# Three attention loops with the turn two blocks behind the scores and projection steps shared out one by one

## What is computed

```python
s_f = einsum('bhqd,bhkd->bhqk', qf, k_f) * scale_f
s_f = s_f + cf[..., :, None] - cum_f[..., None, :]
p_f = softmax(where(causal, s_f, -inf)); o_f = einsum('bhqk,bhkd->bhqd', p_f, v_f)
s_d = einsum('bhcqd,bhckd->bhcqk', qd, k_d) * scale_d
p_d = softmax(where(causal, s_d, -inf))
a_d = p_d[:, :, 0] - lam * p_d[:, :, 1]; o_d = einsum('bhqk,bhkd->bhqd', a_d, v_d)
```

## Time and profile before

| what | us |
|---|---|
| runs of before | 3536.08 median (3534.78 to 3537.95) |
| profiled execution | 3540.3 |
| its span, first to last instruction | 3538.2 |
| PE busy in it | 3451.2 |
| DVE, ACT, POOL busy | 1223.9, 1256.6, 1522.4 |
| first, second attention loop and third block's loop (scores, first to last) | 1704 to 1869, 2711 to 2876, 3395 to 3501 |

### The profile page before, as it was taken

The page is one execution under the profiler, slowest core; times in us unless marked ns, Lnnn a source line. Parts: engine busy times, 40 slices in busy tenths (PEclk is TensorE's granted clock), DMA queues, the critical chain, the costliest instruction groups (busy, mean ns, idle before and its releaser), DMA issues.

```text
span 3538.2 us, 39182 instructions
## 1 busy us (share of the span) xinstructions
PE 3451.2 (98%) x16124; PEld 2779.6 (79%) x16124; DVE 1223.9 (35%) x2100; ACT 1256.6 (36%) x1924; POOL 1522.4 (43%) x709
## 2 busy tenths in 40 slices
PE   7999999999999999999999999999999999999998
PEld 3777887887888887887777888888887778888776
DVE  3165683631221135212554111121113651111544
ACT  4433323432322332223454222232223553222544
POOL 2422353666444444445414444444445234444332
PEclk8999999999999999999999999999999999999999
DMA  6211133442233323333112223232332122233211
GB/s 231 95 54 54 58 116 101 155 155 89 96 129 135 99 95 131 141 98 102 62 32 88 99 97 95 95 101 96 92 102 87 34 75 89 96 95 99 68 65 54
DMA packets 98719, 341.19 MB, mean 96 GB/s; under 512 B 11308, under 2 KB 11564, under 8 KB 98125
## 3 DMA queue, kind: packets, MB, share of 16 engines
q1 hardware_dynamic: 97632, 334.02, 28.4%
q10 hardware_dynamic: 908, 4.67, 0.3%
HBM read 336.02 MB, written 2.10 MB: 96 GB/s over the span
## 4 chain that ended last, share of the span: by engine, by line
PE 91%; DVE 3%; ACT 3%; POOL 1%; issue 1%; DMA 1%; ACTq 0%; DVEq 0%; POOLq 0%
PE ps L1156 25%; PE ps L1158 25%; PE ps L1157 25%; PE ps L1175 2%; PE ps L1176 2%; PE ps L1177 2%; PE ps L1444 2%; PE ps L1471 1%; PE ps L1457 1%; PE ps L1359 1%; POOL t L2612 1%; PE ps L1230 1%; DMA t<-in_w_f1i 1%; DMA t<-in_xT 1%; DVE t L2102 1%
## 5 line engine op out<-in xcount | busy, mean ns | idle before, releaser
L2612 POOL TENSOR_TENSOR t<-t,t 128x1024 fp32r<-128x1024 f32 (+2 forms) x588 | 1363.7, 2322 | 1792.6 <-ACT t L1539 1791.6
L1156 PE MATMUL ps<-t,t 128*128 128x512 f32 (+1 forms) x4048 | 1606.1, 397 | 22.8 <-POOL t L2612 14.2
L1158 PE MATMUL ps<-t,t 128*128 128x512 f32 (+1 forms) x4048 | 1583.1, 391 | 0.0
L1157 PE MATMUL ps<-t,t 128*128 128x512 f32 (+1 forms) x4048 | 1578.2, 390 | 0.0
L1156 PEld LDWEIGHTS ps<-t,t 128*128 128x128 f32 x4048 | 763.5, 189 | 190.6 <-issue 18.8
L1158 PEld LDWEIGHTS ps<-t,t 128*128 128x128 f32 x4048 | 762.1, 188 | 167.3
L1157 PEld LDWEIGHTS ps<-t,t 128*128 128x128 f32 x4048 | 763.1, 189 | 157.6 <-issue 1.4
L1539 ACT CAST t<-t 128x1024 fp32r<-128x1024 f32 (+2 forms) x588 | 583.9, 994 | 567.5 <-PE ps L1158 423.1
L2405 DVE TENSOR_TENSOR t<-t,ps 128x512 f32<-128x512 f32 x110 | 75.7, 688 | 528.9 <-PE ps L1158 514.0
L1606 ACT CAST t<-t 128x512 fp32r<-128x512 f32 x158 | 97.0, 621 | 404.0 <-DVE t L2405 358.2
L1793 ACT ACTIVATE t<-t 128x512 f32<-128x512 f32 x88 | 55.6, 632 | 317.9 <-DVE t L2398 317.8
(11 more groups left out here) (282 smaller groups left out, 2357.0 us busy)
## 6 DMA issues: line engine op xcount, KB each, us to landing
t<-in_w_f1i SPq DMA_DIRECT2D x88, 512.0 KB, 3.3
t<-in_w_f2i SPq DMA_DIRECT2D x88, 512.0 KB, 3.3
t<-in_w_ada SPq DMA_DIRECT2D x72, 512.0 KB, 4.5
t<-in_w_ffi SPq DMA_DIRECT2D x44, 512.0 KB, 3.7
t<-in_w_f1o SPq DMA_DIRECT2D x32, 512.0 KB, 3.5
t<-in_w_f2o SPq DMA_DIRECT2D x32, 512.0 KB, 3.5
t<-in_w_gate SPq DMA_DIRECT2D x24, 512.0 KB, 3.9
t<-in_w_out SPq DMA_DIRECT2D x48, 256.0 KB, 2.7
```

Of the source, the lines that this page charges most:

```text
L1156: e.matmul(out, wh[:, at], X.hi[c][:, 0:N], start=c == first, stop=False)
L1157: e.matmul(out, wh[:, at], X.lo[c][:, 0:N], start=False, stop=False)
L1158: m = e.matmul(out, wl[:, at], X.hi[c][:, 0:N], start=False, stop=c == final)
L2612: e.tensor_tensor(k.WL[:, n % NHL, 0:w], k.raw[:, j % NRAW, 0:w], f(k.WH[:, n % NHL, 0:w]), ALU.subtract).then_inc(*k.rest.inc(('rest', j) ...
```

## The change

In `attend`, for pairs (Fox and third block), one iteration becomes: weigh (scored-1), scores (n), turn of every weighed job up to two behind the scores, a step of `beside`, gather of what was turned, and a second step when `due` allows. `due` grows by `rate` per iteration, 1.0 in the second block and 1.6 in the third, and by 2.0 after the last scores. The number of jobs by which the turn lags is 1 behind the weighed in this phase and 0 after the last scores. For differential heads the branches are written anew. At the crossing to Fox heads the two waiting differential turns come before one step, and up to four gathers after it.

The second yield of each `outd` tile is dropped. In GLA `outer` becomes `outers`: for both directions it first takes the banks and waits for keys and values, and then emits the two matmuls.

```diff
@@ -664,7 +664,7 @@
         self.N = ring(k, 'N ' + tag, k.tmp[3:], since) if tag != 'm' else None
         first = 1 if tag == 'm' else 0
         self.stats = ring(k, 'stats ' + tag, [k.sm[:, 8 * i:8 * i + 8] for i in range(first, first + 8)], since)
-        self.out = 0
+        self.out, self.rate = (0, 1.6 if tag == 'm' else 1.0)
 
     def parts(self, h):
 
@@ -702,35 +702,45 @@
 def attend(on, at, beside):
 
     scored = weighed = turned = gathered = 0
-    total = len(at.jobs)
-    pair = lambda j: at.jobs[j][0][0] != 'd'
-    while gathered < total:
-        if scored < total and pair(scored):
-            if weighed < scored:
-                on.weigh(at, *at.jobs[weighed])
-                weighed += 1
-            on.scores(at, *at.jobs[scored])
-            scored += 1
-        elif scored < total:
-            on.scores(at, *at.jobs[scored])
-            scored += 1
-        if turned > gathered and (pair(gathered) or turned - gathered > 1 or scored == weighed == turned):
+    total, due = (len(at.jobs), 0.0)
+
+    def gather(until):
+        nonlocal gathered
+        while gathered < until:
             h, qt = at.jobs[gathered]
             on.gather(at, h, qt)
             gathered += 1
             if qt == 3:
                 on.head_out(at, h)
                 at.out += 1
-        if weighed < scored and (scored == total or scored - weighed > 1):
+    while gathered < total:
+        pair = scored == total or at.jobs[scored][0][0] != 'd'
+        if pair and weighed < scored:
             on.weigh(at, *at.jobs[weighed])
             weighed += 1
-        two = turned < total and pair(turned)
-        if two:
-            next(beside, None)
-        if weighed > turned and (two or weighed - turned > 2 or scored == weighed):
+        if scored < total:
+            on.scores(at, *at.jobs[scored])
+            scored += 1
+        if not pair:
+            gather(turned - 1)
+            if scored - weighed > 1:
+                on.weigh(at, *at.jobs[weighed])
+                weighed += 1
+        lag = 2 if not pair else 1 if scored < total else 0
+        while turned < weighed - lag:
             on.turn(at, *at.jobs[turned])
             turned += 1
-        next(beside, None)
+        if not pair:
+            next(beside, None)
+            continue
+        due += at.rate if scored < total else 2.0
+        if due >= 1.0:
+            due -= 1.0
+            next(beside, None)
+        gather(turned)
+        while due >= 1.0:
+            due -= 1.0
+            next(beside, None)
     for _ in beside:
         pass
 
@@ -801,7 +811,6 @@
         for n in range(KT):
             on.T(('outd_' + L, n), 'out' + L, n, at.OA, kt=4, first=4)
             on.part(res, n, ('outd_' + L, n))
-            yield
             yield
 
     def norms():
@@ -1330,8 +1339,7 @@
     def chain_begin(self, h):
         for v in range(2):
             self.take(self.k.banks, 'bo', h, v, hold=True)
-        for d in range(2):
-            self.outer(h, 0, d)
+        self.outers(h, 0)
 
     def intra(self, h):
         k, e = (self.k, self.e)
@@ -1344,8 +1352,8 @@
 
     def chain(self, h, step):
         k, e = (self.k, self.e)
-        for d in range(2 if step < 6 else 0):
-            self.outer(h, step + 1, d)
+        if step < 6:
+            self.outers(h, step + 1)
         for d in range(2):
             c = step if d == 0 else 7 - step
             at = slice(64 * c, 64 * c + 64)
@@ -1363,14 +1371,18 @@
         for v in range(2):
             self.k.banks.let(('bo', h, v))
 
-    def outer(self, h, step, d):
-        k, e = (self.k, self.e)
-        c = step if d == 0 else 7 - step
-        p, w = (64 * (c % 2), 256 * (h % 2))
-        b = self.take(k.banks, 'kv', h, step, d)
-        self.wait_ge('kd', h, d)
-        self.wait_ge('value', h // 2, c // 2)
-        e.matmul(b[:, 0:256], k.KD[p:p + 64, d, c // 2, :], k.VT[p:p + 64, c // 2, w:w + 256], start=True, stop=True).then_inc(*k.filled.inc(('filled', ('kv', h, step, d))))
+    def outers(self, h, step):
+
+        k, e, w = (self.k, self.e, 256 * (h % 2))
+        both = []
+        for d in range(2):
+            c = step if d == 0 else 7 - step
+            both.append((d, c, self.take(k.banks, 'kv', h, step, d)))
+            self.wait_ge('kd', h, d)
+            self.wait_ge('value', h // 2, c // 2)
+        for d, c, b in both:
+            p = 64 * (c % 2)
+            e.matmul(b[:, 0:256], k.KD[p:p + 64, d, c // 2, :], k.VT[p:p + 64, c // 2, w:w + 256], start=True, stop=True).then_inc(*k.filled.inc(('filled', ('kv', h, step, d))))
 
     def head_scale(self, s, h):
         sq = head_sum(self.k, h)
```

## The result

The kernel after takes 3565.57 us, median of four runs (3561.73 to 3568.49), against 3536.85 (3534.78 to 3537.95) for the kernel before run beside it: ratio 1.0081 [1.0069, 1.0093], 28.7 us slower. The forecast was 3546, with a range up to 3559: right in its direction, a third of the size. A second measurement of the same kernel gave 3562.89, 25.6 slower. The profiled execution took 3561.73 with a span of 3559.6, 21.4 more than the span before.

A forecast was written before the change was run, and what follows sets the result against it. The prediction took TensorE (PE), busy 98% of the span, as the bound. Two layers at +4.4 us each and the third block at +1.6 added 10.4 to the median of 3536.1, giving 3546, range 3530 to 3559.

The forecast's parts named there:

- steps A, B, C: Layers 0 and 1, three generator steps without PE work: each gather waits for ACT's copies, losing 2.15, 2.1 and 3.1 us.
- The loop end: End of each attention loop: the second copy starts only after the first gather, 1.0 us lost each.
- head silus: Third block: four head silus stand before a needed exp and copy, 10.6 against PE's 8.8, costing 1.7 us.
- Step 3: Lower granted clock after the dense waits of the layers' empty steps: 1.0 us of slowed work per layer, bounds 0 to 3.
- Step 6: Pair steps of each attention: fewer switches between matmul kinds save about 0.08 us a step, -1.0 per attention.
- Steps 4 and 5: Layers: normalisation roots in Fox steps 0.7 us, small waits of covered steps 1.1, crossing from differential to Fox heads 0.4.
- step D: Layers 0 and 1, last in the worked chain of the empty steps: 0.3 us lost.
- The crossing: From differential to Fox heads, four gathers in one go over two T buffers: 0.4 us.
- step 7: Third block: steps without projection, clock, head silus, scans (1.0), small waits, loop end and others sum to 15.5 against 13.9, +1.6 us.
- Every gather waits: Rival: latencies eat the covered steps' margin, 0.5 us at 37 steps adds 18 less 4 already counted; 3560, chance 0.13.
- Only the ends count: Rival: exps do not hold copies in empty steps, which cost as before; -13.7 us together, 3522, chance 0.12.
- Cancelled: Rival: steps without projection lose less, 5.1 us a layer and 8.0 in the third block; together -1.5, 3535, chance 0.30.

The follow-up runs named there:

- e2: Kernel after, with the gather of a step without projection work put off until after the next scores; 3546.79 us, ratio 1.0027.
- e4: Kernel after, with 12 matmuls of unused result put into each of a layer's three empty steps; 3553.60 us, ratio 1.0050.
- e1: Kernel after, with GLA's outer products back in the old order, one wait and one matmul at a time; 3566.04 us, ratio 1.0080.
- e3: Kernel after, with the last weighing issued ahead of the extra projection step; 3556.05 us, ratio 1.0056.
- e9: Kernel after, with the edits of e2 and e3 together; 3541.31 us, ratio 1.0012.

## Why the prediction failed in size

*Right.* The bound (PE), the direction, and the hand-worked chain of the empty steps: steps A, B, C were priced 2.15, 2.1 and 3.1 and measured 2.2, 2.2 and 3.0 in the first layer, 2.2, 2.2 and 2.6 in the second. That a reordering moves only what PE stands still was not right: its busy time rose by 11.4 us. e2 and e4, one moving the gather and the other covering it, confirm that this chain is the cause. The loop end was 1.1 for 1.0; the gather behind the silus lost 5.6 by spacing for 6.6, the next 1.2 for 1.6, the one before 2.7 for 2.5, head silus 2.3 for 1.7. The outer products did nothing (e1).

*Step 3, the clock, was the term that failed most*: 1.0 a layer with 3 as its bound. In the first trace the slowed scores, turns and projection step behind step C lost 3.3 and those between A and B 0.6, so 3.9; the same count gives 3.6 in the second layer, and e4's stages 3.7 and 3.6. I had read that the clock held through the old onset, where 3.2 were lost, and scaled from there. In the first layer 3.4 us at half clock came behind the first wait and 6.8 behind the third, in the second 10.2 in one piece, starting right behind the gather that the second wait held. In the third block the term was 1.0 and by spacing some 2.0 were lost behind the silus.

*A step was missing*: the last turn behind the last weighing behind the addition of the extra step, 1.9 in each of three loops (e3, e9). I had listed what the additional step issues on PE and ACT, and for DVE only the silus and scans.

*Step 6, fewer switches (-1.0 an attention), did not come.* The turns did get shorter by 0.07 a step, but the projection step before a gather ends with 0.32 instead of 0.23 and costs 2.92 instead of 2.86, so some 0.02 a step is left.

*Steps 4 and 5 were charged for the wrong things.* The roots (0.7), the small waits (1.1) and step D's 0.3 cost nothing: between the crossing and the empty steps, and from 1852 to the last scores, no gather waits. The crossing cost more than its 0.4; of its four gathers over two T buffers the second pair waits for a copy, and the largest spacing there is 1.18 for 0.11. Timeline of PE:

```profile
1785.12 1.27 PE L1483 MATMUL ps<-t,t 128*128 128x128 f32 x10
...
1787.30 1.38 PE L1483 MATMUL ps<-t,t 128*128 128x128 f32 x10 [0.91 <-ACT t L1849]
```

A layer by what was measured: 7.4 + 3.9 + 1.9 + 1.1 (loop end) + 1.1 (crossing) - 0.1 = 15.3, less 6.4, is +8.9; the stages say +9.0 and +8.4. The third block: 2.7 + 5.6 + 1.2 for its steps without projection, 2.3 head silus, 2.0 clock, 1.9 last turn and 1.1 loop end make 16.8 against 13.9, so +2.9; the stage says +2.5.

*The rivals.* "Every gather waits" named the nearest time (3560) by a mechanism that is refuted: of the steps with a projection, in which it wanted 0.5 at 37 places, one gather alone is late, the one behind the head silus, which was priced for itself. "Only the ends count" and "Cancelled" needed the empty steps to lose 3.2 and 5.1; they lost 7.4.

*The sum of spans against medians.* Layers and third block give 19.9 of the 21.4 us by which the spans differ. The median difference of 28.7 is larger since the profiled execution of after was its fastest, 3.8 below its median, and that of before 3.5 above. The repeat makes it 25.6. The 19.9 alone would give some 3557, still inside the range up to 3559; the other 6 to 9 us of the medians have no cause shown. The slower executions of after had the lower mean granted clock (0.983 at 3561.73, 0.981 at 3567.79), but only the fastest was profiled, so where they lost time stays open.

*The two rules.* Timeline of ACT at the silus of the third block in after, beside the earlier trace rows:

```profile
3484.54 1.28 ACT L1943 ACT_TABLE_LOAD   x1
3485.84 2.19 ACT L1943 ACTIVATE t<-t 128x512 f32<-128x512 f32 x4
3487.94 1.12 ACT L1618 CAST t<-t 128x512 fp32r<-128x512 f32 x2
3489.07 1.28 ACT L1842 ACT_TABLE_LOAD   x1
3490.37 0.78 ACT L1842 ACTIVATE t<-ps,t 128x512 f32<-128x512 f32 x1
```

Both loads cost 1.30 to the next start, as in the row before. By the 2.66 us a switch of the Trainium skill, "ScalarE: Activation LUTs", What ACT_TABLE_LOAD costs, this gather would have come an estimated 2.7 later than it did; this trace disagrees with it. The lock of the Trainium skill, "SBUF — State Buffer", 🔬 SBUF: two separate sides, by which the loser of VectorE and GpSimd blocks for the whole instruction, this trace can't try: in the third block of the kernel before three weighings took 2.3 to 2.5 us beside a POOL split, one of them, and in the kernel after none takes over 0.49, since next to no POOL work runs beside them. So the 1.0 of step 7 for scans came to nothing, and what a split would have cost in the new order stays open.

## What to carry to other kernels

When a step is moved, list what it puts on *every* in-order queue, and ask what ready work now stands behind an instruction that needs the moved step's own result; here an addition on DVE held a weighing that was otherwise ready. A step without TensorE work must not be the only cover of anything: with the turn two behind the scores the kernel lost 26 us with empty steps, and gained 5 to 9 once these were merged into full ones, the gather had the next scores to hide behind and the loop's end was reordered; of these only the moved gather was tested alone (18 of the 26). Price a cluster of short waits on TensorE with its clock as well, from a stretch that is as dense, not from one half so.

## What the hardware showed unexpectedly

- Useless work made the kernel faster: 72 matmuls more, median 9.3 us less, the two layers' stages 1.7 to 3.3 us less each, granted clock 1.00 (2.4 GHz) instead of 0.81 over the 36 us.
- Half clock (0.50, 1.2 GHz) came in stretches of 3.4 to 20.5 us around three stops of PE of 2 to 3 us within some 16 us. The order of the empty steps alone does not fix its length: in the four kernels that have it alike (after, its repeat, e1, e3) a layer had between 10 and 20 us of it, and the same layer took 206.3 with 10 us (after) and 209.1 with 20 (e1). Waits of 1.1 and 2.1 in the same place (e2) brought 3 us or none.
